# Half of the paged keys' scores woven into the input projection's second half

## What is computed

```
h = rmsnorm(x) * g;  u = h @ w_in                     # 1056 tokens x 1024 @ 1024 x 3584
qa, ka, va, za, xb, ob, zb = split(u)                 # 7 parts of 512 columns
a  = diff_attend(qa, ka, va)                          # 4 heads, two maps each: softmax1 - lam*softmax2
     prompt: causal over 1024 tokens; sample: over 16 pages of 128 keys per sequence, and the 4 new ones
bo = mlstm_scan(conv(xb), ...) * sigmoid(ob) ...      # in chunks, carries a matrix state
y  = concat(norm(a)*silu(za), bo*silu(zb)) @ w_out;  x += norm(y)
x += norm(sigmoid(x @ ple_gate) * (p @ ple_w))
```

## Time and profile before

| | |
|---|---|
| timed executions | 994.46, 994.59, 997.62 us; median 994.59 |
| the profiled execution | 990.42 us, span 988.8 us, mean granted clock 0.967 |
| PE busy | 885.8 us, 90% |
| DVE, ACT, POOL busy | 519.3, 357.9, 142.8 us |
| DMA | 142.48 MB, mean 144 GB/s |

### The profile page before, as it was taken

The page is one execution under the profiler, slowest core; times in us unless marked ns, Lnnn a source line. Parts: engine busy times, 40 slices in busy tenths (PEclk is TensorE's granted clock), DMA queues, the critical chain, the costliest instruction groups (busy, mean ns, idle before and its releaser), DMA issues.

```text
span 988.8 us, 20256 instructions
## 1 busy us (share of the span) xinstructions
PE 885.8 (90%) x8003; PEld 706.4 (71%) x8003; DVE 519.3 (53%) x1067; ACT 357.9 (36%) x777; POOL 142.8 (14%) x306
## 2 busy tenths in 40 slices
PE   3999989999999999997676677789979999999996
PEld 3989979999888888886344445556658786677774
DVE  4634845555474455454677788645564443533223
ACT  5533253443334643344222222335553222421211
POOL 1300000000000000004212123233421000000000
PEclk9999999999999999999789799999989999999998
DMA  7362215222332222224857578689985521203221
GB/s 219 104 173 65 65 57 137 65 65 65 102 107 70 81 84 67 64 65 159 302 197 224 180 248 296 242 281 354 358 317 190 185 86 70 65 26 124 75 91 43
DMA packets 111801, 142.48 MB, mean 144 GB/s; under 512 B 9735, under 2 KB 75911, under 8 KB 111706
## 3 DMA queue, kind: packets, MB, share of 16 engines
q1 hardware_dynamic: 101466, 107.62, 33.8%
q0 software_dynamic: 10240, 33.56, 9.4%
HBM read 125.34 MB, written 15.41 MB: 142 GB/s over the span
## 4 chain that ended last, share of the span: by engine, by line
PE 76%; DVE 10%; DMA 5%; issue 3%; ACT 3%; POOL 1%; SPq 1%; POOLq 0%; ACTq 0%; DVEq 0%
PE ps L2012 71%; PE ps L2015 4%; DVE Kr L1740 3%; DMA Kr<-in_cache_k 2%; DMA Vr<-in_cache_v 2%; DVE pp L1826 2%; DMA xrow<-in_x_prompt 1%; DVE pp L1829 1%; PE ps L2007 1%; ACT wh L997 0%; POOLq L838 0%; DVE st L1840 0%; ACT junk L1273 0%; DVE pp L1842 0%; ACT whi L956 0%
## 5 line engine op out<-in xcount | busy, mean ns | idle before, releaser
L2012 PE MATMUL ps<-hhi,whi 128*128 128x272 f32 (+1 forms) x672 | 228.3, 340 | 1.1 <-DVE hlo L1338 1.1
L2012 PE MATMUL ps<-hhi,wlo 128*128 128x272 f32 (+1 forms) x672 | 218.8, 326 | 0.0
L2012 PE MATMUL ps<-hlo,whi 128*128 128x272 f32 (+1 forms) x672 | 218.4, 325 | 0.0
L2012 PE MATMUL ps<-wh,r 128*128 128x512 f32 (+1 forms) x544 | 155.5, 402 | 0.7 <-DVE wout_lo L1892 0.6
L2012 PEld LDWEIGHTS ps<-hhi,whi 128*128 128x128 f32 x672 | 128.6, 191 | 13.9 <-issue 3.7
L2012 PEld LDWEIGHTS ps<-hlo,whi 128*128 128x128 f32 x672 | 128.7, 192 | 9.9 <-issue 1.9
L2012 PEld LDWEIGHTS ps<-hhi,wlo 128*128 128x128 f32 x672 | 128.4, 191 | 9.2
L2012 PEld LDWEIGHTS ps<-wh,r 128*128 128x128 f32 (+1 forms) x544 | 99.4, 185 | 27.3 <-issue 1.9
L1354 DVE TENSOR_TENSOR wlo<-wst,whi 128x1024 fp32r<-128x1024 f32 x56 | 68.8, 1229 | 81.9 <-ACT whi L956 81.9
L1740 DVE STREAM_TRANSPOSE Kr<-Kr 128x1024 f32<-128x1024 f32 x64 | 76.4, 1225 | 16.3 <-DMA Kr<-in_cache_k 16.3
L753 POOL TENSOR_TENSOR small<-small 128x1 f32<-128x1 f32 (+2 forms) x37 | 8.2, 222 | 494.1 <-ACT junk L1273 198.3
(11 more groups left out here) (362 smaller groups left out, 1310.5 us busy)
## 6 DMA issues: line engine op xcount, KB each, us to landing
wst<-in_w_in SPq DMA_DIRECT2D x56, 512.0 KB, 3.8
Kr<-in_cache_k SPq DMA_DIRECT2D x64, 256.0 KB, 5.4
Kr<-in_cache_k POOLq DMA_DIRECT2D x64, 256.0 KB, 6.0
Vr<-in_cache_v SPq DMA_DIRECT2D x32, 256.0 KB, 4.9
Vr<-in_cache_v POOLq DMA_DIRECT2D x32, 256.0 KB, 6.0
Kr<-in_cache_v SPq DMA_DIRECT2D x32, 256.0 KB, 6.5
Kr<-in_cache_v POOLq DMA_DIRECT2D x32, 256.0 KB, 6.3
out_y_prompt<-rows SPq DMA_DIRECT2D x16, 512.0 KB, 2.8
```

The costliest lines, as they stand in the source:

```text
L2012: return nc.tensor.matmul(out, lhsT, rhs, start=start, stop=stop, **more)
```

## The change

- The key steps of batch 0 (steps 0 to 31, rounds 0 to 7, sequences 0 to 3), `scores_out(0)` and its exponential move from the attention stage into the projection's second half, between chunk 3 and chunk 4 (the exponential into chunk 4). Their pages land in a buffer of their own, `window_keys`, over tiles of U1 that are written later; their scores take banks 4 to 7.
- The gap between chunks 3 and 4 becomes: `fill(1)`, `finish(3)`, `fill(2)`, `q_spread`, `fill(2)`, `new_scores`, `fill(2)`, then eight times `scores(g)`, `fill(2)`. Chunks 4 to 7 keep 33 half-pieces of cover in place of 44.
- A round's four page pairs are issued one by SP and three by GpSimd, in place of two and two. This holds for all 16 rounds.
- SP holds weight tiles 31 and later behind the first pages, and issues one weight tile between rounds.
- `KEY_SHARE` goes from 0.45 to 0.32: steps 32 to 67 are spread over the first 32% of the attention's positions, values over the rest. Several buffers move (`S0`, `vtok`, `AO`, `qk`, two tiles of w_out, the gate weights in three DMAs in place of two); the first value pages are issued at steps 57 to 66 in place of 49 to 64.

```diff
+FILLS = [...] + [(1, 0, 2, 2, 1, 1, 1), (1, 1, 3, 1, 1, 1, 1), (1, 1, 2, 1, 1, 1, 1), (1, 1, 2, 1, 1, 1, 1)]
+WINDOW = (1, 2, 2, 2)
+PER_ROUND = 2
-KEY_SHARE = 0.45
+KEY_SHARE = 0.32
...
 # SP
+            sp.wait_ge(s["ptab_in"], PTAB_IN)
+            sp.wait_ge(s["bo_done"], H)
+            sp.wait_ge(s["wqkv_in"], 64 + 64)
+            key_pages(0)
+            key_pages(ROUND)
+            for w in range(NT + 3, NT + 6):
+                load_w(w)
+            for g in range(2, IN_ROUNDS):
+                key_pages(ROUND * g)
+                load_w(NT + 4 + g)
...
 # GpSimd
             for i in range(H):
                 chunk(i)
+            pool.wait_ge(s["ptab_in"], PTAB_IN)
...
+            def key_pages(n):
+                turn = 3 * (n // ROUND) + n % ROUND - 1
+                if turn % 4 == 0:
+                    own_pages(32 + GP * turn)
...
+            def round_pages(g):
+                for n in range(ROUND * g + 1, ROUND * g + ROUND):
+                    key_pages(n)
...
+            pool.wait_ge(s["bo_done"], H)
+            pool.wait_ge(s["wqkv_in"], 64 + 64)
+            round_pages(0)
+            nc.gpsimd.memset(qk[0][:], 0.0).then_inc(s["zero_ready"], 1)
+            round_pages(1)
             pool.wait_ge(*done["q_rep_stored"])
             own_queries(0)
...
 # the eight instructions that write q_new follow, as before
+            for g in range(2, IN_ROUNDS):
+                round_pages(g)
+            for i in range(H, CH):
+                chunk(i)
...
 # VectorE
+            fill(WINDOW[1])
+            dve.wait_ge(s["piece_done"], 2 * NT)
+            nc.vector.tensor_copy(xb_new[:, :, :], ...)
+            fill(WINDOW[2])
+            new_scores_out()
+            conv_second(0)
+            fill(WINDOW[3])
+            for g in range(IN_ROUNDS):
+                for n in range(ROUND * g, ROUND * g + ROUND):
+                    keys_turned(n)
+                if g + 1 < H:
+                    conv_second(g + 1)
+                fill(PER_ROUND)
+            scores_out(0)
...
 # TensorE
             for i in range(H):
                 chunk(i)
-            fill()
+            fill(WINDOW[0])
             finish(H - 1)
-            fill(11)
+            fill(WINDOW[1])
+            pe.wait_ge(s["C_done"], H)
+            # q_spread, as it stood behind the chunks
+            fill(WINDOW[2])
+            new_scores()
+            fill(WINDOW[3])
+            for g in range(IN_ROUNDS):
+                scores(g)
+                fill(PER_ROUND)
+            pe.wait_ge(s["s_stored"], 4)
```

More of the change, by code:

```diff
@@ L556, in _ @@
             for turn in range(2):
[L557 to L560, removed]
                 for b in range(BATCHES):
@@ L707, in _ @@
             gate_w = io["ple_gate_w"][0].rearrange("(k p) n -> p k n", p=P)
-            for n in range(2):
-                put("wgate_in", wgate[n][:, :, :], gate_w[:, n * half_k:(n + 1) * half_k, :])
+            for (first, n, _), part in zip(wgate_parts, wgate):
+                put("wgate_in", part[:, :, :], gate_w[:, first:first + n, :])
             put("plew_in", plew[:, :, :], io["ple_w"][0].rearrange("(k p) n -> p k n", p=P))
@@ L1256, in _ @@
                     wh_part(WH_AT[pos])
-                for n in range(DECODED[pos - 1] if pos else 0, DECODED[pos]):
+                for n in range(DECODED[pos - 1] if pos else IN_BATCH, DECODED[pos]):
                     decode(n)
@@ L2253, in chunk, with new_scores, scores @@
                 fill(after)
+            def new_scores():
+                pe.wait_ge(s["q8_ready"], NSEQ + 4 * PACK)
+                for b in range(BATCHES):
+                    for h in range(H):
+                        last = mm(ps[32 * h:32 * h + 32, 5, SMP * b:SMP * (b + 1)], q_new[:, b, h, :], tok(KA + h, SEQ, SMP))
+                last.then_inc(*signal["new_scored"])
+            def scores(g):
+                b, r = divmod(g, IN_ROUNDS)
+                j, half = divmod(r, 2)
+                pe.wait_ge(s["k_turned"], ROUND * (g + 1))
+                if g == 0:
+                    pe.wait_ge(*done["new_stored"])
+                    pe.wait_ge(s["bo_done"], H)
+                if r == 0:
+                    pe.wait_ge(s["q8_ready"], NSEQ + 2 * PACK * (1, 3)[b])
+                pages = slice(GROUPS * half, GROUPS * half + GROUPS)
+                for c in range(H):
+                    for h in range(H):
+                        for a in range(4):
+                            rows = slice(32 * a, 32 * a + 32)
+                            first = h * DH + 32 * c
+                            last = mm(ps[32 * h:32 * h + 32, score_bank(b, a), 256 * half:256 * half + 256].rearrange("p (g t) -> p g t", t=32),
+                                      qk[b][rows, j, h, c, :], key_ring(IN_BATCH * b)[rows, pages, first:first + 32],
+                                      r == 0 and c == 0, r == IN_ROUNDS - 1 and c == H - 1, skip_group_check=True)
+                last.then_inc(s["scores_ready"], 1)
@@ L2255, in _ @@
             for i in range(H):
                 chunk(i)
-            fill()
+            fill(WINDOW[0])
             finish(H - 1)
-            fill(11)
+            fill(WINDOW[1])
+            pe.wait_ge(s["C_done"], H)
+            for c in range(H):
+                for a in range(4):
+                    last = mm(ps[32 * a:32 * a + 32, 4, c * P:(c + 1) * P], ident[:, 32 * c:32 * c + 32],
+                              tok(slice(QA, QA + H), SEQ, SMP))
+            last.then_inc(*signal["q_spread"])
@@ L2267, in _ @@
-            last.then_inc(*signal["q_spread"])
             finish(CH - 1)
```

303 lines of the change are left out of this document (143 added, 160 removed).

## The result

The changed kernel takes 1055.19 us (median of four, 1053.59 to 1056.34) against 994.53 for the kernel before in the same comparison: ratio 1.0605, 95% interval 1.0575 to 1.0636. It is 61 us slower. I had said 988, between 973 and 1004: wrong in sign, and outside the range.

The account below looks back on a forecast made before the run. TensorE was taken to bound the projection, and VectorE in program order the attention's key steps. The projection pays 44.2 us, the attention gives back 50.5: 994.6 - 6.3, about 988 us, range 973 to 1004.

Parts of the forecast that it names:

- the fourth item of what the projection pays: Window rounds 1 to 3: VectorE's 9.1 us against 8.2 on TensorE costs 2.4 us; rounds 4 to 7 don't wait.
- the clock: Projection window: half-pieces after 12 us of standing may run at 1.20 GHz; 1 us taken, bounds 0 and 3.
- Rival 4: Projection window: stalls before the first four rounds lower TensorE's clock; +8 or above, 1003 us; chance 0.04.
- GpSimd's chain in front of `new_scores`: Projection window: TensorE stands still until GpSimd has issued pages and laid out `q_new`; 11.8 us.
- VectorE before round 0: Projection window: VectorE's mask sum, conv_second, rest and four turns take 9.5 us against 5.5 of half-pieces; 4.0 us stall.
- The ring: Projection window: page issue, landing and turn, 11.3 to 13.8 us, just fit TensorE's 13.7 us; 0.5 us.
- rival 2: Projection window: GpSimd's queue paces the page ring without slack, late landings cost time; +7, about 1001 us; chance 0.20.
- Thinner cover: Chunks 4 to 7: with fewer half-pieces TensorE comes too early for ScalarE's gate rows; 1 us.
- Before unit 0: Start of attention: fewer key steps, no wait for `q_new`, no `q_spread` before the last turn; gives back 4.5 us.
- Units 0 to 7: Attention: 15 fewer key turns, less waiting around `scores_out` and for key pages; gives back 23.5 us.
- Units 8 to 10: Attention: 12 key and a few value steps become 12 value steps, 39.2 us to 26.2; gives back 13 us.
- Rival 3: Attention: the heads' own chain takes the place, waits for `pp L1826` grow by a third; -1, 994 us; chance 0.13.

Follow-up runs that it names:

- Experiment 1: The changed kernel with the key turns of each window round put ahead of the conv_second and rests covering the round before: 1015.23 us, ratio 1.0227 to the kernel before.
- experiment 2: The changed kernel with one half-piece more ahead of the first window round and one less behind the last chunk: 1016.65 us, ratio 1.0222 to the kernel before.
- Experiment 3: The changed kernel with page pairs issued two by SP and two by GpSimd again: 1057.2 us, ratio 1.0649 to the kernel before.
- experiment 12: experiment 8 with only weight tile 31 ahead of the first pages, tile 32 behind round 0's pages, and KEY_SHARE 0.26: 983.12 us, ratio 0.9899 to the kernel before.
- experiments 1 to 4: The first four follow-up runs, the fourth being the kernel before with the 1:3 page split alone (998.29 us); the kernel before had a median of 993.07 us beside them.
- experiment 8: The changed kernel with its window order mended, page pairs two and two, weight tiles 31 and 32 ahead of the first pages: 993.51 us, ratio 0.9997 to the kernel before.
- experiment 9: experiment 8 with KEY_SHARE at 0.45 in place of 0.32: 990.79 us, ratio 0.9969 to the kernel before.

## Why the prediction was wrong

**The step that failed** is the fourth item of what the projection pays: "Rounds 1 to 3: VectorE has a `conv_second`, a rest and four turns, 9.1 us, against 2.76 + 5.5 = 8.2 on TensorE: 3 x 0.8 = 2.4 us. Rounds 4 to 7 need 5.8 us of it and don't wait for VectorE." It adds up VectorE's work and compares it with the cover. Measured: seven waits of 4.7 us, with a `conv_second` in front as without. The rest can't begin before ScalarE's split, the split not before the tile's second half-piece is through, the half-piece not before the round; and the turns stand behind. That chain is 10.4 us long and has 5.5 us of cover. I counted the rest as 1.2 us of work and asked neither what it waits for nor which of a tile's two half-pieces follows a round. Experiment 1 takes the order away and with it 33 us of waits, experiment 2 the parity and most of them. Of the 54.6 us by which the projection missed, this step is 33.0 - 2.4 = 30.6 directly; the clock, which followed from it, is another 17.7 (12.0 + 6.7 against 1), if the 6.7 left over are the clock's.

**The clock.** Rival 4 had a chance of 0.04 because "from round 4 on there is no stall". Its mechanism was right and its condition was the failed step: with a stall in front of each round the window had 0.83. Its price was 12.0 us on the rounds (I had 14) and up to 6.7 on half-pieces. In experiment 1, with the stalls away, the later rounds have 1.00. So it added to the error and did not start it.

**GpSimd's chain in front of `new_scores`**: forecast 11.8, measured 9.4. The mechanism was right, two terms were too large: the second register load shows as a gap of 0.85 us where I had 2.5, and GpSimd was past its wait for the page table at 271.2 and not at 273. The two together are 3.4 us; the forecast missed by only 2.4 because TensorE was there earlier too, at 278.2 and not at 279.7.

**VectorE before round 0**: forecast 4.0, measured 6.1. The size is near and the cause another: tile 31, issued among the pages, was split at 290.34, and `new_scores_out`, `conv_second(0)` and the turns stood behind its rest. I had named the moved loads in the change and not priced them.

**The ring**: forecast 0.5. Experiment 3 shows the same 39.0 us with another split, and in experiment 12 the rounds come every 8.4 us with 0.6 us of waits for turns. It fits, and rival 2 was wrong for the window. In the attention stage the queue does show. The longest wait for turns there, 9.5 us, ends at 635.60. GpSimd's timeline of the changed kernel, then VectorE's and TensorE's:

```profile
620.12 2.30 POOL L871 DMA_DIRECT2D Kr<-in_cache_k  x4 [2.51 <-issue]
622.77 2.30 POOL L871 DMA_DIRECT2D Kr<-in_cache_k  x4 [0.35 <-issue]
627.58 1.13 POOL L871 DMA_DIRECT2D Kr<-in_cache_k  x2 [2.51 <-issue]
```

```profile
631.98 1.25 DVE L1784 STREAM_TRANSPOSE Kr<-Kr 128x1024 f32<-128x1024 f32 x1 [4.55 <-DMA Kr<-in_cache_k]
```

```profile
635.60 4.08 PE L2073 MATMUL ps<-Kr,qk 32*32 32x256 f32 x128 [9.48 <-DVE Kr L1784]
```

VectorE waits for pages, and GpSimd's issues have two gaps of 2.51 us between them, about as long as a register load took in the earlier trace rows.

**Thinner cover**: forecast 1, measured 3.3 for the gate rows I had named, and 4.5 in places that I had passed over, the largest `S L1799` (2.6), the last scores' way out of their banks behind the last rests.

**What the attention gives back.** Before unit 0: forecast -4.5 (the parts that I priced, 2.4 and 2.5, make 4.9), measured +0.6 (27.6 against 27.0): the wait for `q_new` went, but TensorE waits 4.7 us for ScalarE's `ktok`. Units 0 to 7: forecast -23.5, measured -17.2 (92.9 against 110.1), with 14.4 us of waits for turns left in the attention, against 23.3. Units 8 to 10: forecast -13, measured -14.0. The rest: forecast -9.5, measured -7.0 (109.0 against 116.0, both to the end of the heads). Rival 3 is in this: the waits for `pp` grew from 16.4 to 20.2 us, by a quarter. These four terms miss by 12.9 us together, the projection by 54.6. No experiment takes the 12.9 apart: their cause stays open.

**Was the trade sound?** By little. With the order right the projection pays 34.0 us (experiment 12), of which the rounds and moved work are 23.5, and the attention gives back 42.0; a part of this is `KEY_SHARE`, for at 0.32 the whole was level (experiment 8) and at 0.45, the value of the kernel before, 0.3% faster (experiment 9). The kernel before was not run with another `KEY_SHARE`, so how much of the 1.0% it could have had without the change is not known. By the ratios, the change as it stands lost the trade to some 38 us of order on VectorE (1.0605 to 1.0227) and some 23 us of order elsewhere (1.0227 to 0.9997): on the queues, and on VectorE in front of round 0 and behind the last round.

## What to carry to other kernels

When work is woven into another stage, sums of busy time against the cover say too little. For each instruction that stands in front of the new work on its engine, follow what it waits for, back to the last thing that the new work itself delays: if that path leads through the new work, it is a loop with a length, and the length must be under the cover. Then issue the inputs of the next period ahead of the old work of this one, and a load that a chain needs soon ahead of the many that can wait.

## What the runs showed of the hardware

A load of 512 KB, issued while 16 pages of 256 KB were being issued around it, took 14.1 us to land; the quickest of the three in that stretch took 3.7. Its issue took 0.6 us at most. The Trainium skill ("DMA: Bandwidth & Descriptors", "Issuing engines are not separate DMA queues") says that transfers from all issuing engines run on the same DMA engines and interleave. The row agrees: the tile came from SP, and twelve of the pages from GpSimd. The quickest was issued at 292.3, when those pages had landed.

A round of 128 small matmuls took 2.75 to 2.76 us at a clock of 1.00 where TensorE had idled 0.6 us or less before it (the first three rounds of experiment 12), and 4.03 to 4.53 at 0.50 to 0.63 behind 4.7 us of idle time. The gap right before a round does not decide it alone: in experiment 2 a round behind 2.91 us of idle time took 2.76 us, and one behind 2.03 took 4.05.

Executions of one kernel on one chip lie up to 13 us apart (the kernel before, beside experiments 1 to 4: 988.5 to 1001.4), and the slowest have a lower mean clock than the fastest: in experiment 8 from 987.8 us at 0.971 to 999.0 us at 0.959.
